# A fused two-block transformer kernel: in the first attention ScalarE copies and swaps the rotation's input, values are turned in banks of their own, and one wait moves behind three projections

## What is computed

```python
proj = rms_norm(h, ln_mix_g) @ w_in
qa, ka, va, qb, kb, vb, ga, gb = split(proj)
qa, ka = rope(qa, pos), rope(ka, pos)  # [x1*cos - x2*sin, x2*cos + x1*sin]
ya = dilated_mixture(qa, ka, va) @ w_branch_a   # 3 groups of 4 heads, dilations 1, 4, 16
yb = stick_breaking(qb, kb, vb) @ w_branch_b    # 8 heads of 64
h = h + (sigmoid(ga) * ya + sigmoid(gb) * yb) @ w_out
```

## Time and profile before

| what | us |
|---|---|
| median of three runs (lowest, highest) | 3408.4 (3396.68, 3410.1) |
| the profiled execution, its own time | 3397.45 |
| its span, first to last instruction | 3395.6 |
| TensorE busy in the span | 3062.9 |
| mean granted clock of TensorE | 0.932 of full speed |

### The profile page before, as it was taken

One profiled execution on the slowest core, in us unless ns is written; L12 is line 12 of the kernel. 1 busy time (PEld: TensorE's weight loads), 2 busy tenths in 40 slices (PEclk: granted clock), 3 DMA queues, 4 the chain that ended last, 5 costly groups with the idle time before them and its releaser, 6 DMA issues.

```text
span 3395.6 us, 37913 instructions
## 1 busy us (share of the span) xinstructions
PE 3062.9 (90%) x13994; PEld 2395.6 (71%) x13994; DVE 1530.1 (45%) x1750; ACT 835.5 (25%) x1344; POOL 739.6 (22%) x486
## 2 busy tenths in 40 slices
PE   7789897999999998879999999988999999677888
PEld 6678785665577776657777777777877777566667
DVE  1446554445533344334333333334155454566663
ACT  2101013556610002022111111112143232233441
POOL 4020201222233321102323323221301102100015
PEclk8699998999999998889999999998999999788899
DMA  4210100000021110001111111112110001000023
GB/s 137 87 37 8 44 13 19 19 13 13 11 94 43 45 48 19 25 13 38 44 49 43 43 49 43 49 37 81 32 27 13 20 1 38 1 6 5 0 87 118
DMA packets 166187, 128.67 MB, mean 38 GB/s; under 512 B 14945, under 2 KB 150913, under 8 KB 165809
## 3 DMA queue, kind: packets, MB, share of 16 engines
q1 hardware_dynamic: 164528, 118.55, 11.6%
q10 hardware_dynamic: 1536, 8.54, 0.7%
HBM read 114.20 MB, written 12.65 MB: 37 GB/s over the span
## 4 chain that ended last, share of the span: by engine, by line
PE 62%; DVE 7%; issue 2%; ACT 2%; DMA 1%; SPq 0%; ACTq 0%; DVEq 0%
PE ps L653 15%; PE ps L654 14%; PE ps L655 14%; PE ps L2198 7%; PE ps L580 2%; PE ps L2255 1%; PE ps L2256 1%; PE ps L2257 1%; PE ps L2333 1%; PE ps L2334 1%; PE ps L2335 1%; DVE dX L1565 1%; DVE dF L1754 1%; PE ps L597 1%; PE ps L2155 0%
## 5 line engine op out<-in xcount | busy, mean ns | idle before, releaser
L653 PE MATMUL ps<-NH,w_high 128*128 128x512 f32 (+1 forms) x2048 | 810.2, 396 | 125.6 <-DVE qM_low L1846 39.0
L654 PE MATMUL ps<-NL,w_high 128*128 128x512 f32 (+1 forms) x2048 | 810.1, 396 | 0.0
L655 PE MATMUL ps<-NH,w_low 128*128 128x512 f32 (+1 forms) x2048 | 805.4, 393 | 0.0
L925 POOL CAST w_high<-w_raw 128x1024 fp32r<-128x1024 f32 x193 | 204.1, 1058 | 2464.9 <-PE ps L655 1291.0
L653 PEld LDWEIGHTS ps<-NH,w_high 128*128 128x128 f32 x2048 | 395.2, 193 | 224.3 <-issue 110.8
L927 POOL TENSOR_TENSOR w_low<-w_raw,w_high 128x1024 fp32r<-128x1024 f32 x193 | 470.0, 2435 | 15.5
L655 PEld LDWEIGHTS ps<-NH,w_low 128*128 128x128 f32 x2048 | 394.6, 193 | 86.9
L654 PEld LDWEIGHTS ps<-NL,w_high 128*128 128x128 f32 x2048 | 394.6, 193 | 86.8
L708 DVE TENSOR_TENSOR hT<-hT,ps 128x1024 f32<-128x1024 f32 x168 | 205.1, 1221 | 249.2 <-PE ps L655 249.2
L1722 DVE TENSOR_TENSOR probs_low<-probs,probs_high 128x512 fp32r<-128x512 f32 (+4 forms) x224 | 133.3, 600 | 84.0 <-ACT probs L1217 81.0
L1215 ACT ACTIVATE probs_high<-ps 128x512 fp32r<-128x512 f32 (+4 forms) x224 | 112.9, 504 | 230.7 <-PE ps L2198 191.2
(11 more groups left out here) (344 smaller groups left out, 5163.6 us busy)
## 6 DMA issues: line engine op xcount, KB each, us to landing
w_raw<-in_w_in SPq DMA_DIRECT2D x69, 512.0 KB, 3.8
w_raw<-in_w_up SPq DMA_DIRECT2D x44, 512.0 KB, 3.8
w_raw<-in_w_out SPq DMA_DIRECT2D x24, 512.0 KB, 3.6
w_raw<-in_w_down SPq DMA_DIRECT2D x22, 512.0 KB, 3.8
x_in<-in_x SPq DMA_DIRECT2D x8, 512.0 KB, 5.7
w_raw<-in_w_xkv SPq DMA_DIRECT2D x8, 512.0 KB, 4.1
residual_spill<-hT SPq DMA_DIRECT2D x1, 4096.0 KB, 12.5
hT<-residual_spill ACTq DMA_DIRECT2D x1, 4096.0 KB, 12.8
```

Source lines behind the costliest of these rows:

```text
L653: nc.tensor.matmul(o, wh, xh, start=start, stop=False)
L654: nc.tensor.matmul(o, wh, xl, start=False, stop=False)
L655: return nc.tensor.matmul(o, wl, xh, start=False, stop=stop)
L925: nc.gpsimd.tensor_copy(WH[slot][:, :], w_raw[slot][:, :]).then_inc(w_high, 1)
```

## The change

Per projection Q or K of attention A, ScalarE now copies the 1024 columns of PSUM to `plain` (`hT` chunk 5) and frees the slot, then copies `plain` to `swap` (`hT` chunk 4) in four instructions of 32 rows, each to the neighbouring 32 rows. VectorE multiplies `plain` by the cosines and `swap` by the sines, one instruction each, and subtracts. V0 and V1 are turned into banks 6 and 7 (`turned_v`) and are no jobs any more; V2 still is. The wait for `s_set` moves behind the first three projections of SB, into the loop.

```diff
-    A_JOBS = list("wwwwxwwwxwwx") + ["o"] * 6
+    A_JOBS = list("wwwwwwwwwx") + ["o"] * 6
...
+        turned_v = ps[:, 6:8, :].rearrange("p a b -> p (a b)")
...
# ScalarE
+                for g in range(A_GROUPS):
+                    for x in range(2):
+                        n, k = 6 * p + 2 * g + x, 3 * g + x
+                        wait_done(act, A, 0, k)
+                        if n:
+                            act.wait_ge(a_q, n)
+                        nc.scalar.activation(plain[:, :], pair[A.slot(k)], ACT.Copy).then_inc(job_free[A.slot(k)], 1)
+                        wait_freed(act, A, 0, k)
+                        if (p, k) == (1, 0):
+                            act.wait_ge(a_y, 1)
+                        for q4 in range(4):
+                            o, s_ = 32 * q4, 32 * (q4 ^ 1)
+                            nc.scalar.activation(swap[o:o + 32, :], plain[s_:s_ + 32, :], ACT.Copy).then_inc(a_swap, 1)
+                    dil, k = A_DIL[g], 3 * g + 2
                     wait_done(act, A, 0, k)
+                    if g:
+                        act.wait_ge(a_turn, 2 * p + g)
...
# VectorE, rope
-                nc.vector.tensor_tensor(rot1[:, :], x, cos_a[:, :], ALU.mult)
-                for q4 in range(4):
-                    o, s_ = 32 * q4, 32 * (q4 ^ 1)
-                    r = nc.vector.tensor_tensor(rot2[o:o + 32, :], x[s_:s_ + 32, :], sin_a[s_:s_ + 32, :], ALU.mult)
-                link(r)
-                nc.vector.sem_inc(job_free[A.slot(k)], 1)
+                nc.vector.tensor_tensor(rot1[:, :], plain[:, :], cos_a[:, :], ALU.mult)
+                dve.wait_ge(a_swap, 4 * n + 4)
+                rot2 = swap
+                link(nc.vector.tensor_tensor(rot2[:, :], rot2[:, :], sin_a[:, :], ALU.mult))
...
-                                                rot2[rows, :].rearrange("p (a r) -> p r a", r=dil), ALU.add)
+                                                rot2[rows, :].rearrange("p (a r) -> p r a", r=dil), ALU.subtract)
...
# TensorE
+                for n in range(9):
+                    proj(n, n)
+                    if n in (3, 6):
+                        turn_values(n // 3 - 1)
+                pe.wait_ge(a_vfree, 2 * p + 2)
...
-            pe.wait_ge(s_set, 1)
             with pe.Fori(0, SB.iters) as i:
...
                     wait_freed(pe, SB, i, J + 1)
+                    pe.wait_ge(s_set, 1)
                     scores(0)
```

More of the change, by code:

```diff
@@ L329, in program @@
         rot1 = acc_u = hT[:, 3, :]
-        rot2 = acc_d = hT[:, 4, :]
+        swap = acc_d = hT[:, 4, :]
+        plain = hT[:, 5, :]
         qA[2] += [hT[:, 6 + h, :] for h in range(2)]
@@ L474, in program @@
         out_ready, out_stored = sem("out_ready"), [sem(f"out_stored{n}") for n in range(2)]
+        a_swap, a_turn, a_vfree = (sem(x) for x in ("a_swapped_ready", "a_values_turned", "a_values_taken"))
         a_rows = [sem(f"a_row_landed{n}") for n in range(2)]
@@ L995, in _ @@
                 A = st_a[p]
-                for g, k in enumerate((2, 6, 10)):
-                    dil = A_DIL[g]
+                for g in range(A_GROUPS):
[12 more added lines that the diff above has]
+                    dil, k = A_DIL[g], 3 * g + 2
                     wait_done(act, A, 0, k)
+                    if g:
+                        act.wait_ge(a_turn, 2 * p + g)
                     nc.scalar.activation(vtmp[:, :].rearrange("p (r a) -> p r a", r=dil),
@@ L1010, in _ @@
                             act.wait_ge(a_row, 2 * p + h)
-                        wait_done(act, A, 0, 11)
+                        wait_done(act, A, 0, 9)
                         for g in range(A_GROUPS):
@@ L1355, in _, with rope @@
             dve.wait_ge(rope_in, 32)
[L1357 to L1360, removed]
-                nc.vector.tensor_tensor(rot1[:, :], x, cos_a[:, :], ALU.mult)
-                for q4 in range(4):
-                    o, s_ = 32 * q4, 32 * (q4 ^ 1)
-                    r = nc.vector.tensor_tensor(rot2[o:o + 32, :], x[s_:s_ + 32, :], sin_a[s_:s_ + 32, :], ALU.mult)
-                link(r)
-                nc.vector.sem_inc(job_free[A.slot(k)], 1)
+            def rope(A, p, k, dst, g):
+                dil, n = A_DIL[g], 6 * p + 2 * g + k % 3
+                wait_freed(dve, A, 0, k)
+                nc.vector.tensor_tensor(rot1[:, :], plain[:, :], cos_a[:, :], ALU.mult)
+                dve.wait_ge(a_swap, 4 * n + 4)
+                rot2 = swap
+                link(nc.vector.tensor_tensor(rot2[:, :], rot2[:, :], sin_a[:, :], ALU.mult))
                 for to, rows in dst:
@@ L1369, in rope, with values @@
                                                 rot1[rows, :].rearrange("p (a r) -> p r a", r=dil),
-                                                rot2[rows, :].rearrange("p (a r) -> p r a", r=dil), ALU.add)
+                                                rot2[rows, :].rearrange("p (a r) -> p r a", r=dil), ALU.subtract)
                 link(r)
                 nc.vector.sem_inc(a_q, 1)
-            def values(A, k, g):
-                wait_done(dve, A, 0, k)
+            def values(A, p, g):
+                if g < 2:
+                    dve.wait_ge(a_turn, 2 * p + g + 1)
+                    src, taken = turned_v, a_vfree
+                else:
+                    wait_done(dve, A, 0, 9)
+                    src, taken = pair[A.slot(9)], job_free[A.slot(9)]
                 nc.vector.tensor_copy(vA[g][:, :, :].rearrange("p t (s d) -> p t s d", s=3)[:, :, 0:3:2, :],
-                                      pair[A.slot(k)].rearrange("p (t s d) -> p t s d", s=2, d=HD))\
-                    .then_inc(job_free[A.slot(k)], 1)
+                                      src.rearrange("p (t s d) -> p t s d", s=2, d=HD)).then_inc(taken, 1)
             def maxima(A, h, g, u, unit):
@@ L1431, in _ @@
                 A = st_a[p]
[L1432 to L1439, removed]
+                rope(A, p, 0, q_dst(0), 0)
+                rope(A, p, 1, k_dst(0), 0)
+                rope(A, p, 3, q_dst(1), 1)
+                values(A, p, 0)
+                rope(A, p, 4, k_dst(1), 1)
+                rope(A, p, 6, q_dst(2), 2)
+                values(A, p, 1)
+                rope(A, p, 7, k_dst(2), 2)
                 seq = a_order()
@@ L1445, in _ @@
                     elif what[0] == "vt2":
-                        values(A, 11, 2)
+                        values(A, p, 2)
                     elif what[0] == "mt":
@@ L1452, in _ @@
                         dve.wait_ge(a_pv, 20 * p + what[4] + 1)
-                        gather(A, 12 + 3 * what[1] + what[2], what[1], what[2])
+                        gather(A, 10 + 3 * what[1] + what[2], what[1], what[2])
                 link(nc.vector.reciprocal(acc_d[:, :], acc_d[:, :]))
@@ L1940, in proj, with turn_values @@
                         dense2(pe, A, 0, 0, 0, NORM["mix"][2])
-                def turn_values(k, g):
-                    wait_freed(pe, A, 0, (2, 6, 10)[g])
-                    wait_pair(pe, A, 0, k)
-                    for t in range(NT):
[L1946 to L1951, removed]
+                def turn_values(g):
+                    wait_freed(pe, A, 0, 3 * g + 2)
+                    if g < 2:
+                        if 2 * p + g:
+                            pe.wait_ge(a_vfree, 2 * p + g)
+                        to, done = turned_v, a_turn
+                    else:
+                        wait_pair(pe, A, 0, 9)
+                        to, done = pair[A.slot(9)], job_done
+                    for t in range(NT):
+                        mm = nc.tensor.transpose(to[:, t * P:(t + 1) * P], vtmp[:, t * P:(t + 1) * P], ident)
+                    mm.then_inc(done, 1)
+                for n in range(9):
[3 more added lines that the diff above has]
+                pe.wait_ge(a_vfree, 2 * p + 2)
                 for what in a_order():
@@ L1971, in _ @@
                     elif what[0] == "vt2":
-                        turn_values(11, 2)
+                        turn_values(2)
                     elif what[0] == "mt":
@@ L2002, in _ @@
                         _, h, g, u, n, unit = what
-                        k = 12 + 3 * h + g
+                        k = 10 + 3 * h + g
                         if u == 0:
                             wait_pair(pe, A, 0, k)
-                            wait_freed(pe, A, 0, (4, 8, 11)[g])
+                            if g < 2:
+                                pe.wait_ge(a_vfree, 2 * p + g + 1)
+                            else:
+                                wait_freed(pe, A, 0, 9)
                         m = p * 20 + n
```

## The result

The changed kernel took 3347.67 us in the median of four runs (3342.7 to 3355.55), the one before 3406.39 us (four runs). Ratio **0.9839, 95% interval 0.982 to 0.9859**: 1.6% faster, 58.7 us between the medians. The forecast of 3350 us (3334 to 3370) holds.

The account below looks back on a forecast made before the run. TensorE, busy 3062.9 us, bounds the kernel, so only its waits and low-clock time can be won. Gains of 30.1 + 5.4 + 16.7 = 52.2 us from 3397.45 give 3345.2 (3356 by the high level); forecast 3350 us, range 3334 to 3370.

Parts of the forecast that it names:

- Part 1: Attention A: K1 and K2 no longer wait for slots, four blocked passes going from 78.08 to 48.00 us; gain 30.1 us.
- Part 2: V0 of p = 0 starts at about 151.6 instead of 156.99, limited by its weights and GpSimd's split; gain 5.4 us.
- Part 3: SB's first projection no longer waits for `s_set`: 14.85 us of waiting plus 1.88 us of clock; gain 16.7 us.
- the 1.88 us of clock: SB's first pass: low clock after the 17.27 us gap costs 1.88 us, nearly nothing after a 2.43 us gap.
- The cover of SB's V: SB: Q's slot is free at about 535.5, V wants to start at 539.5; covered by 4 us.
- The sum: Whole kernel: 30.1 + 5.4 + 16.7 = 52.2 us, giving 3345.2 us against the profiled execution's 3397.45.
- two levels: Whole kernel's run times: 3345.2 us by the low level, 3356 by the high; forecast taken between them.
- 1, the clock falling at the turns: Four turns between projections: the clock falls at 1.88 us each, giving back 7.5 us, 3352.7 us; chance 0.05.
- 2: V0 of p = 0: its weights are no limit and the pass starts at 144.9, 3338.5 us; chance 0.05.
- 3: SB: its first wait is only replaced by another and the 16.7 us come back, 3361.9 us; chance 0.09.
- 4: Attention A: ScalarE's 32-row copies set the pace, kernel slower; at 4.2 us each 17 us slower, 3414; chance 0.02.
- the formula: Attention A: chain per group 12.1 + 8X, X per 32-row copy, hidden up to X = 2.8, losing from X = 3.85.

Follow-up runs that it names:

- the two single-part kernels: The kernel before with only V0 and V1 turned in banks 6 and 7: ratio 0.9907; with only ScalarE's copies, swaps and the new rotation: 0.9882.
- V0's weights first: The changed kernel with the DMA of V0's weights issued ahead of the spill: 3347.93 us, ratio 0.9841 to the kernel before.

## Why the prediction was right

**Part 1, K1 and K2: right.** Forecast 12.00 us from Q's end to K's; ScalarE's copies are 12.02, 12.02, 12.00 and 12.00 us apart in the changed kernel (188.66 - 176.64 and its three likes), against 78.08 us together before. Gain 30.0. What the prediction put too narrowly is the cause. Its first paragraph names both conditions, the slot and the rotation that has just begun, but part 1 gives all of the gain to the turns' slots. The copies alone do the same, as the two single-part kernels show, so the sentence "the turns leave the slots" was sufficient and not necessary.

**Part 2, V0: right within a microsecond.** Forecast start 151.6, measured 151.39. The gap is 8.93 us here, 10.19 in the changed kernel run again, 10.32, 9.62 and 9.48 in three others that start V0 the same way, against 14.60: a gain of 4 to 6 us for the 5.4 forecast. The limit named, GpSimd's low part behind a late DMA, is the releaser in the row, and moving the DMA moved the start by 7 us.

**Part 3, SB: the 14.85 us of waiting right, the 1.88 us of clock only in some executions.** The stretch puts the part at 17.0 us alone, and at 15.1 (390.5 - 375.4) and 16.8 (390.5 - 373.7) as the last part of three, for 16.7. The rows at the place itself are cleaner. The gap shrank from 17.27 to 2.34 us, for 2.43, in every execution with the moved wait. From SB's Q to the transposes of its V are 568.43 - 531.81 = 36.62 us before, 34.77 in the changed kernel and 36.30 in its second execution, where the clock fell again. So the part was worth 16.8 us in the first and 15.3 in the second. The cover of SB's V held: VectorE's low part of Q starts at 499.51 and takes 2.46 us, and no wait ahead of V is in the view of waits.

**The sum: 52.2 forecast, 50.7 and 52.4 measured** over the stretch in two executions. The medians differ by 58.7 us and the profiled executions by 41.9, because of scatter outside the stretch: of the profiled pair, 8.7 us are lost behind SB's first V (stretches from there to the end of 2827.2 and 2835.9 us). That, and the 1.5 us by which the stretch fell short of the sum, is why the profiled execution came out 10 us above the 3345.2 of the prediction's sum. The instructions behind that V are the same in all eleven profiles, and they took from 2825.4 to 2839.6 us. In the seven kernels with the moved wait they took 2830.8 to 2839.6, in the four without it 2825.4 to 2834.0, so one profile each does not rule out that the moved wait gives some microseconds back later. The ratios do not bear that out: they put the moved wait at 23.5 us alone and at about 19 as the last part (0.9895 - 0.9839), not below 17. Here is one piece of the scatter, an attention stage of the second block, with the same 867 matmuls (length, busy time of PE, PEld, DVE, ACT, POOL, granted clock, DMA), before:

```profile
2698.00:2876.00 178.00, 170.18 (x867) 133.72 (x867) 96.76 (x137) 63.88 (x131) 22.47 (x14) 0.99 0.08 18
```

and after:

```profile
2648.00:2832.00 184.00, 176.21 (x867) 138.73 (x867) 97.80 (x137) 64.45 (x131) 23.57 (x14) 0.95 0.07 17
```

Six microseconds, and the granted clock is 0.99 against 0.95. The "two levels" of the whole time, between which the prediction took a midpoint, are not there: seven runs of the kernel before on one chip took 3396.16, 3397.9, 3400.18, 3401.41, 3406.74, 3407.8 and 3410.2 us. Such drops may be what they are summed from, but that was not followed through the whole kernel. That the median came within 2.3 us of the forecast of 3350 was luck as much as judgement.

**The rivals.** 1, the clock falling at the turns: not so. From 158 to 258 us, with both turns in it, no 2-us slice of the changed kernel is under 1.00, and none from 312 to 432, with the two turns of p = 1. What the Trainium skill says ("TensorE: Matmul & The Clock Gate", Part 4) about transposes not counting as busy had no effect here with 0.9 us of them between full passes. 2 and 3 fell with the experiments above. 4's mechanism is real, but its price was too low: about 33 us at 4.33 us per copy, where the formula gives 23. With the formula's slope of 48 us of loss per microsecond of X the break-even would be 3.6 us instead of 3.85, an estimate from this one point; the real swap, 1.06 us, is under a third of it.

## What to carry to other kernels

When a wait needs two conditions (a shared buffer and a slow release), either remedy removes it and the second brings next to nothing: try the cheaper one alone first. Here that is the order of issue, not 63 us of copies: two free banks, one DMA ahead of a large spill, six memsets behind the work that frees a buffer, and a wait put next to its first user. Measure a small part over a stretch of the trace that holds it; the whole kernel's scatter was as large as the part.

## What the runs showed that was not expected

**VectorE and GpSimd hold each other up when VectorE reads two SBUF tensors.** In the changed kernel the first rotation's products run while GpSimd splits a tile:

```profile
150.40 2.02 DVE L1376 TENSOR_TENSOR hT<-hT,cos_a 128x1024 f32<-128x1024 f32 x1
152.34 2.05 DVE L1379 TENSOR_TENSOR hT<-hT,sin_a 128x1024 f32<-128x1024 f32 x1
154.43 4.50 DVE L1381 TENSOR_TENSOR qA<-hT 64x1024 f32<-64x1024 f32 x2
160.14 1.23 DVE L1376 TENSOR_TENSOR hT<-hT,cos_a 128x1024 f32<-128x1024 f32 x1 [1.21 <-ACT hT L1005]
```
```profile
151.28 2.03 POOL L928 CAST w_high<-w_raw 128x1024 fp32r<-128x1024 f32 x1
153.40 3.22 POOL L930 TENSOR_TENSOR w_low<-w_raw,w_high 128x1024 fp32r<-128x1024 f32 x1
```

2.02 and 2.05 us instead of 1.23 and 4.50 instead of 2.45 on VectorE, 2.03 and 3.22 instead of 1.04 and 2.34 on GpSimd. The rows read as taking turns. GpSimd's cast, begun at 151.28, ends 0.89 us after VectorE's first product (153.31 after 152.42); the second product, begun at 152.34, ends 1.08 us after the cast (154.39); GpSimd's 3.22 us end 2.23 us after that; and VectorE's subtractions end 2.31 us after GpSimd (158.93 after 156.62). Each ends about its own undisturbed length after the other's instruction. Before, the same moment had products out of PSUM (4.92 us for four), at full speed. With V0's weights first, GpSimd was done at 151.00, and of Q0's rotation only the product begun before that was long:

```profile
150.14 1.94 DVE L1378 TENSOR_TENSOR hT<-hT,cos_a 128x1024 f32<-128x1024 f32 x1
152.00 1.21 DVE L1381 TENSOR_TENSOR hT<-hT,sin_a 128x1024 f32<-128x1024 f32 x1
153.25 2.45 DVE L1383 TENSOR_TENSOR qA<-hT 64x1024 f32<-64x1024 f32 x2
```

ScalarE's swaps took 4.29 to 4.31 us in either case. The Trainium skill ("SBUF — State Buffer", Who interferes with whom) says that a VectorE instruction with two SBUF inputs contends with a GpSimd instruction that reads SBUF. These rows agree with it, and the prediction should have used it: its 155.8 for the end of Q0's rotation was 158.9 in the trace. Only the cover (Q1 wanted the slot at 164.5) kept it off the path.

**A gap of 2.3 to 2.5 us costs the clock in some executions and not in others.** Eighteen such gaps ahead of a projection stand in the eleven profiles of this case (2.34 to 2.45 us, the hand-over from attention A's outputs). Behind nine of them the granted clock was 1.00. Behind the other nine it was 0.57 to 0.68 over the first 4 us: it fell to 0.50 within the first half microsecond in eight of them, and 1.4 us after the restart in the ninth (306.09, below). Two of one execution of the changed kernel, four microseconds from each restart:

```profile
306.10:310.10 4.00, 4.00 (x12) 3.17 (x13) 3.94 (x2) 0.00 (x0) 0.00 (x0) 0.67 0.00 0
...
483.00:487.00 4.00, 3.94 (x17) 3.21 (x18) 3.90 (x2) 0.00 (x0) 0.00 (x0) 1.00 0.00 0
```

Each fall takes about 1.5 us (the stretch from SB's Q to its V's transposes is 34.77 us without and 36.30 with it). So "nearly nothing after 2.43 us", in the prediction's first part, was one side of a coin. The same goes for waits of 3.1 to 3.2 us for VectorE's shifts: the changed kernel lost the clock behind the one of p = 1, its second execution did not. What decides it I did not try to find out.
